# Low halves of the first squared-ReLU layer's weights by accumulating DMAs, in a three-pass float32r kernel on one core

## The reference, cut to what matters

```python
def squared_relu_mlp(h, w_up, w_down):      # w_up (1024, 4096), w_down (4096, 1024)
    u = jax.nn.relu(h @ w_up)
    return (u * u) @ w_down
...
h = h + squared_relu_mlp(rms_norm(h, g_mlp[layer]), w_mlp_up[layer], w_mlp_down[layer])
```

## Time and profile before

| what | value |
|---|---|
| median of the runs (2 runs) | 2479.15 us |
| lowest and highest run | 2478.89 and 2479.42 us |
| span of the profiled execution, first to last instruction | 2477.6 us |
| what lies around the span, against the two runs | 1.3 to 1.8 us |
| PE busy, share of the span | 100% |
| DVE, ACT, POOL busy | 56%, 38%, 4% |
| blocks 36 to 89, from the chain of waits | 289.78 to 583.54 us |

### The profile page before, as it was taken

The page is one execution under the profiler, slowest core; times in us unless marked ns, Lnnn a source line. Parts: engine busy times, 40 slices in busy tenths (PEclk is TensorE's granted clock), DMA queues, the critical chain, the costliest instruction groups (busy, mean ns, idle before and its releaser), DMA issues.

```text
span 2477.6 us, 31594 instructions
## 1 busy us (share of the span) xinstructions
PE 2469.6 (100%) x11544; PEld 2029.9 (82%) x11544; DVE 1384.1 (56%) x1762; ACT 952.4 (38%) x1213; POOL 104.0 (4%) x83
## 2 busy tenths in 40 slices
PE   9999999999999999999999999999999999999999
PEld 7888888888888888888888888888777778888887
DVE  5777544344767765544344544545868846544343
ACT  3676433233334343442233323223465453333222
POOL 2000100001000000100002100001000001000000
PEclk9999999999999999999999999999999999999999
DMA  4112332233222222333333232333222223333333
GB/s 140 57 52 60 94 101 93 96 109 109 85 85 77 77 85 85 104 98 93 101 94 95 93 101 93 98 98 110 85 69 69 77 64 98 93 97 98 93 101 111
DMA packets 76061, 225.40 MB, mean 91 GB/s; under 512 B 12240, under 2 KB 22736, under 8 KB 75856
## 3 DMA queue, kind: packets, MB, share of 16 engines
q1 hardware_dynamic: 71744, 222.24, 29.5%
q10 hardware_dynamic: 4240, 2.10, 0.3%
HBM read 222.21 MB, written 2.10 MB: 91 GB/s over the span
## 4 chain that ended last, share of the span: by engine, by line
PE 97%; DVE 2%; issue 0%; DMA 0%; ACT 0%; ACTq 0%; SPq 0%; DVEq 0%
PE ps L2060 54%; PE ps L2065 27%; PE ps L2667 2%; PE ps L2129 2%; PE ps L2113 1%; PE ps L2410 1%; PE ps L2285 1%; PE ps L2242 1%; PE ps L2261 1%; PE ps L2226 1%; PE ps L2397 1%; PE ps L2248 1%; DVE score L1799 1%; PE ps L2644 0%; PE ps L2722 0%; PE ps L2274 0%
## 5 line engine op out<-in xcount | busy, mean ns | idle before, releaser
L578 ACT ACTIVATE w_hi<-raw 128x1024 fp32r<-128x1024 f32 x406 | 430.7, 1061 | 1204.0 <-PE ps L2065 1155.1
L2060 PE MATMUL ps<-x_hi,w_hi 128*128 128x512 f32 x1936 | 761.7, 393 | 0.0
L2060 PE MATMUL ps<-x_lo,w_hi 128*128 128x512 f32 x1936 | 754.0, 389 | 0.0
L1197 DVE TENSOR_TENSOR w_lo<-raw,w_hi 128x1024 fp32r<-128x1024 f32 x406 | 499.8, 1231 | 150.3 <-ACT w_hi L578 150.0
L2065 PE MATMUL ps<-x_hi,w_lo 128*128 128x512 f32 x1936 | 478.2, 389 | 0.0
L2060 PEld LDWEIGHTS ps<-x_hi,w_hi 128*128 128x128 f32 x1936 | 363.5, 188 | 80.6 <-issue 4.0
L2060 PEld LDWEIGHTS ps<-x_lo,w_hi 128*128 128x128 f32 x1936 | 363.6, 188 | 75.5 <-issue 1.7
L2065 PEld LDWEIGHTS ps<-x_hi,w_lo 128*128 128x128 f32 x1936 | 363.4, 188 | 75.6
L2060 PE MATMUL ps<-u_hi,w_hi 128*128 128x512 f32 x858 | 334.3, 390 | 0.0
L2060 PE MATMUL ps<-u_lo,w_hi 128*128 128x512 f32 x858 | 333.9, 389 | 0.0
L1377 DVE SCALAR_TENSOR_TENSOR h<-ps,h 128x512 f32 (+1 forms) x135 | 93.3, 691 | 337.6 <-PE ps L2065 333.3
(11 more groups left out here) (386 smaller groups left out, 2438.7 us busy)
## 6 DMA issues: line engine op xcount, KB each, us to landing
raw<-in_stream SPq DMA_DIRECT2D x413, 512.0 KB, 3.6
x_tok<-in_x SPq DMA_DIRECT2D x4, 512.0 KB, 7.8
out_x<-xn ACTq DMA_DIRECT2D x7, 256.0 KB, 2.3
tab_ret<-in_tables_ret SPq DMA_DIRECT2D x1, 1536.0 KB, 6.5
raw<-in_stream SPq DMA_DIRECT2D x3, 256.0 KB, 3.2
tab_mix<-in_tables_mix SPq DMA_DIRECT2D x1, 384.0 KB, 4.2
prm<-in_params SPq DMA_DIRECT2D x1, 298.5 KB, 4.7
out_x<-xn ACTq DMA_DIRECT2D x2, 128.0 KB, 1.8
```

Source lines behind the costliest of these rows:

```text
L578: nc.scalar.activation(w_hi[:, slot(n)], raw[:, slot(n)], ACT.Copy).then_inc(hi_done, 1)
L1197: nc.vector.tensor_tensor(w_lo[:, slot(n)], raw[:, slot(n)], w_hi[:, slot(n)].bitcast(F32), ALU.subtract).then_inc(lo_done, 1)
L2060: nc.tensor.matmul(ps[:, gemm_bank(n)], w_hi[:, s, k], x(k), start=(k == 0 and i == 0), stop=False)
```

## The change

For 54 blocks, number 36 to number 89 (`ADDED`), the low half is made in another way. ACT first writes w_lo = -raw, rounded to float32r, which is the negated high half, and then w_hi as before. POOL waits for hi_done and issues a DMA that reads raw and adds it onto w_lo, both in SBUF. It waits until that has landed and then raises lo_done itself. DVE leaves these blocks out. SP's loads of the blocks from 38 to 91 are written out in place of a loop, with the same wait. Beside this, four semaphores of the attention layer's query and key splits become two.

```diff
+ADDED = range(RUN_AT["mlp0"] + 4, RUN_AT["ret"] - DC + 2)
...
+def number_in_added(n):
+    return place_of(n)[1] is not None or place_of(n)[0] + 2 in ADDED
...
+            def load_added(n):
+                sp.wait_ge(lo_done, n + 1)
+                sp.dma_start(raw[:, n % 2], stream[n].rearrange("p (k m) -> p k m", m=P)).then_inc(raw_full[n % 2], 16)
-            load_run(RUN_AT["sb_out"], RUN_AT["ret"] - DC)
+            load_run(RUN_AT["sb_out"], ADDED[0] + 2)
+            for n in range(ADDED[0] + 2, RUN_AT["ret"] - DC):
+                load_added(n)
 
             sp.wait_ge(sig("ul_done"), HIDDEN // P)
             sp.dma_start(tab_ret[:], tables_ret).then_inc(sig("tables_in"), 16)
-            load_run(RUN_AT["ret"] - DC, RUN_AT["mlp1"] + DC)
+            for n in range(RUN_AT["ret"] - DC, ADDED[-1] + 3):
+                load_added(n)
+            load_run(ADDED[-1] + 3, RUN_AT["mlp1"] + DC)
...
-            def split_hi(n):
+            def split_hi(n, added=False):
...
+                if added:
+                    nc.scalar.activation(w_lo[:, slot(n)], raw[:, slot(n)], ACT.Copy, scale=-1.0)
                 nc.scalar.activation(w_hi[:, slot(n)], raw[:, slot(n)], ACT.Copy).then_inc(hi_done, 1)
...
-                nc.scalar.activation(q_hi[:, p % 2], sb_q[:], ACT.Copy).then_inc(sig("qh_done"), 1)
+                nc.scalar.activation(q_hi[:, p % 2], sb_q[:], ACT.Copy).then_inc(sig("qkh_done"), 1)
...
-            def split_lo(n):
+            def split_lo(n, added=False):
+                if added:
+                    return
+                if n == ADDED[-1] + 1:
+                    dve.wait_ge(lo_done, n + 2)
...
+            def add_raw(n):
+                s, i = n % 2, n - ADDED[0]
+                pool.wait_ge(hi_done, n + 1)
+                if i == 0:
+                    pool.wait_ge(lo_done, n + 2)
+                nc.gpsimd.dma_start(w_lo[:, s], raw[:, s], accum_op=ALU.add).then_inc(
+                    sig(f"added_{s}"), 16)
+                pool.wait_ge(sig(f"added_{s}"), 16 * (i // 2 + 1))
+                pool.sem_inc(lo_done, 1)
+
             for k in range(len(NORMS)):
+                if k == N_MIX1:
+                    for n in range(ADDED[0], RUN_AT["ret"] - DC + 2):
+                        add_raw(n)
...
-                pe.wait_ge(sig("ql_done"), p + 1)
-                pe.wait_ge(sig("kl_done"), p + 1)
+                pe.wait_ge(sig("qkl_done"), 2 * p + 2)
```

More of the change, by code:

```diff
@@ L661, in q_split @@
                 act.wait_ge(bank_free[slot(query_block(p))], turn(query_block(p), 2))
-                nc.scalar.activation(q_hi[:, p % 2], sb_q[:], ACT.Copy).then_inc(sig("qh_done"), 1)
+                nc.scalar.activation(q_hi[:, p % 2], sb_q[:], ACT.Copy).then_inc(sig("qkh_done"), 1)
             def k_split(p):
                 act.wait_ge(bank_free[slot(query_block(p) + 1)], turn(query_block(p) + 1, 2))
-                nc.scalar.activation(k_hi[:, p % 2], sb_k[:], ACT.Copy).then_inc(sig("kh_done"), 1)
+                nc.scalar.activation(k_hi[:, p % 2], sb_k[:], ACT.Copy).then_inc(sig("qkh_done"), 1)
             def sb_exp(hd):
@@ L726, in two @@
                 def two(n, _):
-                    split_hi(later(n, 2))
-                    split_hi(later(n, 3))
+                    split_hi(later(n, 2), first in ADDED)
+                    split_hi(later(n, 3), first in ADDED)
                 pairs(act, first, blocks, two)
@@ L734, in ahead_of_norm @@
                     for n in split_after(first, c):
-                        split_hi(n)
+                        split_hi(n, n in ADDED)
                     chunk(k, c)
@@ L750, in up @@
                     for i in range(2):
-                        split_hi(later(n, i + 2))
+                        split_hi(later(n, i + 2), first == RUN_AT["mlp0"] and number_in_added(n))
                         if t is None and i == 0 and group == 0:
@@ L1289, in q_split @@
             def q_split(p):
-                dve.wait_ge(sig("qh_done"), p + 1)
+                dve.wait_ge(sig("qkh_done"), 2 * p + 1)
                 nc.vector.tensor_tensor(q_lo[:, p % 2], sb_q[:], q_hi[:, p % 2].bitcast(F32),
-                                        ALU.subtract).then_inc(sig("ql_done"), 1)
+                                        ALU.subtract).then_inc(sig("qkl_done"), 1)
             def k_split(p):
-                dve.wait_ge(sig("kh_done"), p + 1)
+                dve.wait_ge(sig("qkh_done"), 2 * p + 2)
                 nc.vector.tensor_tensor(k_lo[:, p % 2], sb_k[:], k_hi[:, p % 2].bitcast(F32),
-                                        ALU.subtract).then_inc(sig("kl_done"), 1)
+                                        ALU.subtract).then_inc(sig("qkl_done"), 1)
             def sb_softplus(hd):
@@ L1384, in two @@
                         add_product(later(n, i), flat(h[:, at(t, 2, i)]), scale)
-                        split_lo(later(n, i + 2))
+                        split_lo(later(n, i + 2), first in ADDED)
                 if first + blocks == N_RUN:
@@ L1406, in residual_of_norm @@
                     for n in split_after(first, c):
-                        split_lo(n)
+                        split_lo(n, n in ADDED)
                     low(k, c)
@@ L1439, in up @@
                             scaled(later(n, i), u_act[:], 0.0, ALU.max)
-                            split_lo(later(n, i + 2))
+                            split_lo(later(n, i + 2), first == RUN_AT["mlp0"] and number_in_added(n))
                         hidden_lo(t, 2, i, count(t, 2, before + i + 1), group)
```

## The result

The changed kernel takes 2531.64 us (2531.05 to 2532.24), against 2479.15 before: 52.5 us more, a ratio of 1.0212 with a 95% interval of 1.0182 to 1.0242. The forecast was 2545, slower, by the adds that PE waits for. The direction, the place and the mechanism are as forecast; the extra time was put too high by 13 us, 66 where 52.5 was measured.

A forecast was written before the change was run, and what follows sets the result against it. PE, with 97% of the chain, bounds the kernel. With the first add hidden and then 6.7 us a block against 5.44, block 89 comes 66 us late: 2479.15 + 66 = about 2545 us, range 2476 to 2670.

The forecast's parts named there:

- The stage has nothing to give: Blocks 36 to 89: PE runs without gaps, 5.44 us a block, so removing 66.2 us of DVE subtractions gains 0.
- ACT's copy hides: ACT's added negated copy, 1.06 us a block, is covered by 3.1 us of idle time before each w_hi: cost 0.
- Loop 1: POOL handles one add at a time, so a block takes at least D + 0.2 = 6.7 us.
- plain move: Base part of each add's time: a transfer of 512 KB without adding, put at 3.6 us.
- second read: Part of each add's time: reading w_lo besides raw, put at 1.45 us.
- D: Time from hi_done to the add's landing, put at 6.5 us, between 3.6 and 9.8.
- hand-over: Passing from one engine to another, 0.1 to 0.2 us; 0.2 was added to each add in POOL's queue.
- Loop 2: A raw slot's round in two blocks: two copies, add, load and hand-overs; 6.3 to 7.0 us a block.
- Rival A: The adds are hidden behind PE, with D about 5.2 and add plus load 8.4 us: 2479 us; chance 0.28.
- Rival B: The add's reads and write follow one another, D 7.95 and 8.15 us a block: 2625 us; chance 0.22.
- Rival D: A DVE operation of 0.69 us holds up POOL at each add, 7.4 us a block: 2585 us; no separate chance.
- Rival C: PE's pauses drop the granted clock to 1.2 GHz, 10.88 us a block: 2773 us; chance 0.03.

The follow-up runs named there:

- the plain copy: Changed kernel, but POOL's DMA copies raw over w_lo instead of adding, so the low halves are left out: 2479.67 us.
- every second block: Changed kernel, but only the 27 odd blocks are added by DMA and DVE makes the even ones: 2478.9 us, ratio to before 0.9999.
- POOL's wait gone: Changed kernel, but POOL waits for no add to land; SP waits, raises lo_done and issues the next load: 2527.78 us, ratio to before 1.0194.
- small loads: Changed kernel, but the loads of blocks 38 to 91 bring 64 KB in place of 512, adds staying whole: 2481.8 us.
- both edits: Changed kernel, but SP instead of POOL waits for landings, and the add starts after the negated copy, before w_hi: 2490.12 us, ratio to before 1.0043.
- the tables moved: The version with both edits, with the retention tables' load moved behind block 91's load and the last add: 2484.88 us, ratio to before 1.0023.

## Why the prediction was right, and what was mis-sized

*The stage has nothing to give.* Right. DVE fell from 1384.1 to 1322.3 us busy, 61.8 us less, and both runs that hid the POOL DMAs with whole loads (the plain copy, and every second block) came out at the time before or 0.7 us above it, and not under it.

*ACT's copy hides.* Right, shown alone.

*Loop 1, one add at a time.* Right as the binding loop, 6.28 us typically and 6.45 on average against my 6.7. Its terms were off, partly against each other, and that the sum came so close is in part luck:

| term | forecast | measured |
|---|---|---|
| plain move of 512 KB by POOL | 3.6 | 2.9 |
| second read (measured: all that the adding brings) | 1.45 | 1.5 |
| a load beside it | 1.45 | 1.3 to 1.4 |
| D | 6.5 | 5.7 to 5.8 |
| hand-over, landing to next start | 0.2 | 0.57 |

The step that was mis-sized is "a plain move": I took the load from HBM for it, 3.6 us, and gave the source in SBUF no credit, though the 256 KB store in 2.3 us pointed that way; the copy took 2.9. The hand-over failed the other way, since no row showed POOL going from a wait to a DMA: in 0.52 us of it the profile shows no wait, so I take them for POOL's own. Together 6.3 instead of 6.7, 0.4 x 53 = 21 us too much. I left out the table load; the long adds around it, 10.2 and 6.9 us against 5.75, give 5.6 us back, and the first add, early by 1.1 us and not by 0.6, takes 0.5. That, too, is two errors against each other: it started at 287.76 and not at 286.24, since ACT was late with w_hi, and took 4.57 us and not 6.5. From 66: 66 - 21 + 5.6 - 0.5 = 50, where 52.5 was measured; the rest is that ordinary blocks averaged a little over 6.3.

*Loop 2, through raw.* I had it at 6.3 to 7.0, beside loop 1. With POOL's wait gone it was 6.8 us a block in one stretch and 6.0 on average in the rest. That the two are close was right, and it is why one edit did little.

*Rival A, hidden adds.* Its condition was D of 5.2 and D + L of 8.4. An undisturbed add, 4.4 and 3.6, meets both, also with the measured hand-over (4.4 + 0.57 = 4.97). The runs that kept it undisturbed came within 3 us of the time before, one with small loads and one with half the adds. What decides against A is that adds and loads run beside each other. Some of that can't be avoided, since 4.4 + 3.6 = 8.0 us have to go into 5.44; how long it takes at other offsets from the load was not tried by itself. *Rival B* falls: an undisturbed add takes 4.4 us where B has 6.5. *Rival D* falls: POOL's part is the same length each time in the changed kernel (293 to 560 us; length ns min, median, max), whatever DVE does:

```profile
L2051 POOL DMA_DIRECT2D w_lo<-raw x42: 859/859/862, 292.9 to 553.7; - x42
```

*Rival C, the clock.* Not in the regular pauses, but see below. My argument against it was a wrong reading: in the attention layer PE is busy for 72.00 of 72.00 us, so that stretch has no pauses and says nothing on what pauses do.

## What to carry to other kernels

A DMA that adds in SBUF is not a copy: 4.4 us for 512 KB against 2.9, with 1.9 times the engine time. Before moving work from an engine that has slack, write down every loop that the new step lies on (the issuer's queue, each buffer's slot) and compare each with the pace of the bound engine; two loops within a few per cent must be shortened together. And where one completion releases two transfers at once, read the price of each beside the other: here the add went from 4.4 to 5.7 us and the load from 3.6 to 3.8.

## What the runs showed that I had not expected

**The clock fell after one long pause.** From 293 to 598 us PE waited for POOL 47 times, 27.9 us in total and 1.9 us at most, and the granted clock stayed at 1.00. Beside the table load PE waited 5.0 us for one add. Busy time by stretch in the changed kernel (length, then PE, PEld, DVE, ACT, POOL busy, granted clock, DMA share, GB/s), and PE's timeline:

```profile
608.00:612.00 4.00, 1.13 (x5) 0.59 (x4) 0.00 (x0) 1.04 (x2) 0.00 (x0) 1.00 0.97 296
612.00:616.00 4.00, 1.85 (x4) 1.49 (x5) 0.00 (x0) 0.00 (x0) 0.86 (x1) 0.68 0.58 106
616.00:620.00 4.00, 4.00 (x11) 3.12 (x10) 0.69 (x1) 2.00 (x2) 0.00 (x0) 0.50 0.91 225
620.00:624.00 4.00, 4.00 (x19) 3.24 (x18) 0.00 (x0) 0.00 (x0) 0.86 (x1) 0.97 0.65 167
```

```profile
603.37 2.12 PE L2100 MATMUL ps<-u_hi,w_lo 128*128 128x512 f32 x8 [0.58 <-POOLq L2054]
...
614.15 3.78 PE L2100 MATMUL ps<-u_hi,w_lo 128*128 128x512 f32 x8 [5.01 <-POOLq L2054]
```

The clock went to 0.50, the lower level of 1.2 GHz, and came back about six us after PE resumed. Here the next adds covered it. In the version with both edits the chain shows it on the path: 8 low matmuls in 3.78 and 16 high in 4.74 us, behind an add of 8.24. At the full clock the low ones take 2.11 after a wait (at 634.27 in the changed kernel) and the high ones 3.63, so the clock cost 2.8 us:

```profile
565.54 8.24 DMA w_lo<-raw
...
573.87 3.78 PE ps L2100 x8
577.65 4.74 PE ps L2095 x16
582.39 1.81 PE ps L2100 x8
```

The pause that brought the clock down was 3.1 us in this run. With the tables moved, PE had no pause there, the clock stayed at 1.00, and PE's pieces were 3.63 and 1.81 us again. So about half of what the table load cost there was the clock (2.8 us) and half the pause (3.1 us). That is read from one profiled execution of each, and the two differ by 8.0 us where the medians differ by 5.2, so the split is rough.

**What stays open.** Single adds of 6.7 to 7.1 us stand in the series of the changed kernel (at 368.95, 470.85 and 620.89 us), the last one with and without the table load; why was not tried, nor why the version with POOL's wait gone varies by 14 us even between three of its runs. Its two rhythms may take different shares of different runs; this isn't shown, since only one run has a profile.
